# Convolutions moved behind the query/key pairs, temporaries in PSUM, rotations ahead of VectorE's low halves, h scaled pair by pair

## What is computed

```python
qk = jax.nn.silu(causal_conv(qk, c_conv_w[j], c_conv_b[j]))   # 2048 channels, 4 taps
lf = jax.nn.log_sigmoid(fg + c_b_f[j])
yc = mlstm(q, k, v, li, lf)
...
h = h + mix
pl = rmsnorm(p[i] @ ple_w[i], ple_norm[i])
h = h + jax.nn.sigmoid(h @ ple_gate_w[i]) * pl
...
return rmsnorm(h, final_norm)          # input of the second block, also its residual
# second block, both layers
q_b = apply_rope(qkv_b[:, :, 0], rot); k_b = apply_rope(qkv_b[:, :, 1], rot)
return x + (y @ w_out)
```

## Time and profile before

| | us |
|---|---|
| three timed runs | 2450.66, 2452.96, 2455.09 |
| their median | 2452.96 |
| the profiled execution | 2449.15 |
| its span, first to last instruction | 2447.4 |
| PE, POOL, DVE, ACT busy in it | 2223.3, 1801.4, 1354.6, 1230.6 |

### The profile page before, as it was taken

The page is one execution under the profiler, slowest core; times in us unless marked ns, Lnnn a source line. Parts: engine busy times, 40 slices in busy tenths (PEclk is TensorE's granted clock), DMA queues, the critical chain, the costliest instruction groups (busy, mean ns, idle before and its releaser), DMA issues.

```text
span 2447.4 us, 39060 instructions
## 1 busy us (share of the span) xinstructions
PE 2223.3 (91%) x12256; PEld 1899.9 (78%) x12256; DVE 1354.6 (55%) x1915; ACT 1230.6 (50%) x2192; POOL 1801.4 (74%) x1378
## 2 busy tenths in 40 slices
PE   6998885799997999879997889989999999998997
PEld 5887774688886788768886767778888888876886
DVE  6447687634538737774356765443742454258712
ACT  5454354456543455545564335334665544456654
POOL 6884466799877977669996955666679899854695
PEclk9999998899998999999998989999999999999998
DMA  7654332466654554435665433545456665643464
GB/s 241 191 169 121 91 104 68 147 189 190 182 178 140 173 176 134 125 121 168 188 197 153 148 100 114 156 150 160 142 172 188 181 193 172 190 123 109 138 174 135
DMA packets 211097, 378.92 MB, mean 155 GB/s; under 512 B 23440, under 2 KB 34320, under 8 KB 210832
## 3 DMA queue, kind: packets, MB, share of 16 engines
q1 hardware_dynamic: 205056, 363.95, 49.7%
q10 hardware_dynamic: 5904, 13.23, 1.5%
HBM read 374.99 MB, written 2.10 MB: 154 GB/s over the span
## 4 chain that ended last, share of the span: by engine, by line
PE 44%; POOL 20%; DVE 18%; issue 14%; ACT 3%; POOLq 0%; DVEq 0%; DMA 0%; ACTq 0%
PE ps L448 26%; POOL w_lo L401 20%; PE ps L449 13%; PE ps L530 1%; DVE ps L1361 1%; DVE tb L1360 1%; PE ps L698 1%; ACT w_hi L809 1%; DVE w L1366 1%; DVE ob L1602 1%; DVE w L1895 1%; DVE w L1533 1%; DVE w L1449 1%; PE ps L642 0%; DVE xa L1338 0%
## 5 line engine op out<-in xcount | busy, mean ns | idle before, releaser
L401 POOL TENSOR_TENSOR w_lo<-raw,w_hi 128x512 fp32r<-128x512 f32 (+1 forms) x1374 | 1801.2, 1332 | 624.8 <-ACT w_hi L809 586.9
L809 ACT ACTIVATE w_hi<-raw 128x512 fp32r<-128x512 f32 (+1 forms) x1420 | 854.2, 618 | 813.9 <-PE ps L449 761.8
L448 PE MATMUL ps<-xa,w_hi 128*128 128x512 f32 x2960 | 1077.9, 407 | 84.2 <-POOL w_lo L401 34.4
L449 PE MATMUL ps<-xa,w_lo 128*128 128x256 f32 x2960 | 838.2, 283 | 0.0
L448 PE MATMUL ps<-xb,w_hi 128*128 128x512 f32 x2160 | 768.4, 400 | 9.3 <-POOL w_lo L401 7.3
L448 PEld LDWEIGHTS ps<-xa,w_hi 128*128 128x128 f32 x2960 | 567.3, 192 | 232.4 <-POOL w_lo L401 31.9
L449 PE MATMUL ps<-xb,w_lo 128*128 128x256 f32 x2160 | 606.3, 281 | 0.0
L449 PEld LDWEIGHTS ps<-xa,w_lo 128*128 128x128 f32 x2960 | 570.5, 193 | 0.8
L448 PEld LDWEIGHTS ps<-xb,w_hi 128*128 128x128 f32 x2160 | 406.8, 188 | 110.5 <-POOL w_lo L401 8.2
L449 PEld LDWEIGHTS ps<-xb,w_lo 128*128 128x128 f32 x2160 | 409.5, 190 | 0.5
L1360 DVE TENSOR_SCALAR tb<-ps 128x512 f32<-128x512 f32 (+1 forms) x124 | 85.1, 686 | 389.1 <-PE ps L449 387.7
(11 more groups left out here) (307 smaller groups left out, 2086.5 us busy)
## 6 DMA issues: line engine op xcount, KB each, us to landing
raw<-w_gate_dram SPq DMA_DIRECT2D x128, 256.0 KB, 3.0
raw<-w_ogz_dram SPq DMA_DIRECT2D x128, 256.0 KB, 3.0
raw<-w_odin_dram SPq DMA_DIRECT2D x128, 256.0 KB, 3.0
raw<-w_evmoba_dram SPq DMA_DIRECT2D x112, 256.0 KB, 3.1
raw<-w_ein_dram SPq DMA_DIRECT2D x96, 256.0 KB, 3.1
raw<-w_evout_dram SPq DMA_DIRECT2D x80, 256.0 KB, 3.0
raw<-w_odgate_dram SPq DMA_DIRECT2D x72, 256.0 KB, 3.0
raw<-w_ein_zx_dram SPq DMA_DIRECT2D x64, 256.0 KB, 3.0
```

Of the source, the lines that this page charges most:

```text
L401: nc.gpsimd.tensor_tensor(w_lo[:, slot, 0:n], raw[:, at, 0:n], w_hi[:, slot, 0:n].bitcast(F32), SUB).then_inc(lo_pool, 1)
L448: mm(ps[:, bank + b, :], w_hi[:, slot, at], x[:, x0 + k, :], start=(k == 0), stop=False)
L449: ins = mm(ps[:, bank + b, 0:T], w_lo[:, slot, at], x[:, x0 + k, 0:T], start=False, stop=(k == st.blocks - 1))
L809: af(w_hi[:, slot, 0:n], raw[:, at, 0:n], ACT.Copy).then_inc(act_rounded, 1)
```

## The change

The squares of x are made two blocks at a time into PSUM banks 6 and 7, and added by DVE into `sq_sum`; ACT waits for these additions from the fourth on. ACT's eight DMA issues and the Exp for the parameters come later; the root of x comes before the parameter steps, and pair 3 of ein before the series. `root` keeps variance and temporary in PSUM bank 6, Newton has three operations in place of four, and `log1p` keeps two temporaries there, with one more copy. The convolution of a pair follows its take in oqk, with its accumulator in PSUM banks 4 and 5, its sigmoid behind unit 2 two pairs on, and its product behind the take of that pair; nothing of it is left in ov, where the Exp of the gates goes from unit 4 to unit 8. DVE makes no low half in oqk, one (unit 6) a pair in evmoba and odin from pair 2, and in both the rotation of pair p-2 comes first, then the low half, in odin the memory block, then the take. PE's wait for the variance before odin's second pair goes. The two multiplications of h go; in evout each pair of h is scaled by the kept root and `final_norm` in two operations ahead of its addition.

```diff
 LO_DVE = {
-    "oqk": (2, (3, 7)), "evmoba": (1, (3, 7)), "odmem": (0, (3, 7)),
+    "evmoba": (2, (6,)), "odin": (2, (6,)), "odmem": (0, (3, 7)),
 }
...
             def root(name, which):                                   # ACT
                 act.wait_ge(var_ready, ROOTS[name] + 1)
-                af(rs[:, which, :], tb[:, 0, :], ACT.Sqrt).then_inc(std_ready, 1)
+                af(rs[:, which, :], ps[:, 6, 0:T], ACT.Sqrt).then_inc(std_ready, 1)
...
-                if (p, q) in ((0, 5), (0, 7), (1, 0), (1, 1)):
-                    k = 4 * {5: 0, 7: 1, 0: 2, 1: 3}[q]
-                    af(w[:, k:k + 4, :], h[:, k:k + 4, :], ACT.Square).then_inc(sq_ready, 1)
-                if p == 1 and q == 2:
+                j = {(0, 5): 0, (0, 6): 1, (0, 7): 2, (1, 0): 3, (1, 1): 4, (1, 2): 5, (1, 3): 6, (1, 4): 7}.get((p, q))
+                if j is not None:
+                    if j > 2:
+                        act.wait_ge(sq_added, j - 2)
+                    af(spare(6 + j % 2) if j else sq_sum, h[:, 2 * j:2 * j + 2, :], ACT.Square).then_inc(sq_ready, 1)
+                if p == 1 and q == 4:
...
+                if q == 2 and not (isinstance(p, int) and p < 2):    # oqk, ACT
+                    conv_sigmoid(p - 2, par)
...
-            def conv_behind(p, par, q):
+            def mg_behind(p, par, q):                                # ov, ACT
                 if p == 0 and q == 4:
+                    conv_sigmoid(7, 1)
+                if p == 0 and q == 8:
                     act.wait_ge(mg_in, 1)
                     af(w[:, 36, :], w[:, 36, :], ACT.Exp, scale=-1.0).then_inc(mg_exp, 1)
-                if q in (7, 14):
-                    conv_sigmoid(2 * p + q // 14, q // 14)
...
             def newton(r, v, t, told=False):
-                step(tt(t, r, r, MUL))
-                step(tt(t, t, v, MUL))
-                step(ts(t, t, -0.5, 1.5, MUL, ADD))
+                step(tt(t, v, r, MUL))
+                step(stt(t, t, -0.5, r, MUL, MUL))
...
-                    step(tt(r, r, t, MUL))
+                    step(stt(r, t, 1.5, r, ADD, MUL))
...
-            def log1p(y, z, zz, p):
+            def log1p(y, zs, p):
+                n = y.shape[1]
+                z, zz = ps[:, 6, 0:n], ps[:, 6, T:T + n]
...
-                step(tt(zz, z, z, MUL))
+                step(ts(zs, z, 1.0, None, MUL))
+                step(tt(zz, z, zs, MUL))
...
-            for k in (4, 8, 12):
-                dve.wait_ge(sq_ready, k // 4 + 1)
-                step(tt(w[:, 0:4, :], w[:, 0:4, :], w[:, k:k + 4, :], ADD))
-            tt(w[:, 0:2, :], w[:, 0:2, :], w[:, 2:4, :], ADD).then_inc(sq_added, 1)
-            dve.wait_ge(sq_added, 1)
+            for j in range(1, 8):
+                dve.wait_ge(sq_ready, j + 1)
+                tt(sq_sum, sq_sum, spare(6 + j % 2), ADD).then_inc(sq_added, 1)
+                dve.wait_ge(sq_added, j)
+            root("x", RS_LAYER, D)
+            store("ein", w, 0, RS_LAYER, 0, 2)
...
-            root("x", RS_LAYER, D)
-            store("ein", w, 0, RS_LAYER, 0, 3)
+            store("ein", w, 0, RS_LAYER, 2, 3)
+            store("ein", w, 0, RS_LAYER, 3, 4, adding="mem", behind=2)
...
+            def oqk_pair(p, par):                                    # DVE
+                take(ST["oqk"], p, par, w[:, ds(p * 2, 2), :], RS_LAYER)
+                dve.wait_ge(pair_out, p + (STORED["oqk"] + 1))
+                if not (isinstance(p, int) and p < 2):
+                    silu(p - 2, par)
+                convolve(p, par)
+            for p in range(4):
+                oqk_pair(p, p % 2)
+            pairs_loop(dve, 8, oqk_pair, 4, steps=step, per=8)
+            store("ogate", w, 32, RS_LAYER)
+            silu(6, 0)
...
-                convolve(2 * p, 0)
-                if p:
-                    silu(2 * p - 1, 1)
-                convolve(2 * p + 1, 1)
-                silu(2 * p, 0)
...
-            root("first", RS_Q, D)
-            rf, rl, v = rs[:, RS_Q, :], rs[:, RS_LAYER, :], tb[:, 0, :]
-            step(tt(rl, rf, rf, MUL))
-            step(stt(v, ps[:, 7, T:2 * T], 1.0 / D, rl, MUL, MUL))
+            root("first", RS_FIRST, D)
+            rf, rl, v, t = rs[:, RS_FIRST, :], rs[:, RS_LAYER, :], ps[:, 6, 0:T], ps[:, 6, T:2 * T]
+            step(tt(v, ps[:, 7, T:2 * T], rf, MUL))
+            step(stt(v, v, 1.0 / D, rf, MUL, MUL))
...
-            step(tt(h[:, :, :], h[:, :, :], along(rf, 16), MUL))
-            step(tt(h[:, :, :], h[:, :, :], wide(col("final_norm"), 16), MUL))
...
                 def pair(p, par):                                    # results_pair
-                    dst = w[:, ds(p * 2, 2), :]
+                    if nb:
+                        rotate(p + (rope_at - 2), (rope_at + par) % 2, kind, p * 2 - 4, nb)
                     lower(st, p, par)
-                    take(st, p, par, dst, RS_LAYER)
                     if memory_behind:
                         split_gained("mem3", p, par, xb)
-                    if nb:
-                        dve.wait_ge(pair_out, p + STORED[name])
-                        rotate(p + (rope_at - 1), (rope_at + 1 + par) % 2, kind, p * 2 - 2, nb)
+                    take(st, p, par, w[:, ds(p * 2, 2), :], RS_LAYER)
+                    dve.wait_ge(pair_out, p + (STORED[name] + 1))
...
+                    if x_next:                                       # add_out
+                        for b in range(2):
+                            step.post(stt(hp[:, b:b + 1, :], hp[:, b:b + 1, :],
+                                          cols[:, ds(p * 2 + (COL_AT["final_norm"] + b), 1)],
+                                          rs[:, RS_FIRST:RS_FIRST + 1, :], MUL, MUL))
+                        step.wait()
                     a, b = halves_of(st, p, par)
```

More of the change, by code:

```diff
@@ L248, in build @@
         NORMS, n, m = {}, 0, 0
-        for name, squares, additions in (("x", 4, 1), ("mem", 8, 7), ("ple0", 2, 1), ("h1", 8, 7), ("ple1", 2, 1),
+        for name, squares, additions in (("x", 8, 7), ("mem", 8, 7), ("ple0", 2, 1), ("h1", 8, 7), ("ple1", 2, 1),
                                          ("first", 16, 14), ("cq", 2, 1), ("ckv", 1, 0), ("x3", 8, 7), ("last", 8, 7)):
@@ L1111, in conv_behind @@
                     af(small[:, 0:16], ps[:, 7, 0:16], ACT.Copy).then_inc(mg_gcols, 1)
-            stage("oqk", peel=2, behind=oqk_behind)
-            stage("ogate")
-            stage("ov", behind=conv_behind, peel=4)
+            stage("oqk", peel=4, behind=oqk_behind)
+            stage("ogate", behind=lambda p, par, q: conv_sigmoid(6, 0) if q == 2 else None)
+            stage("ov", behind=mg_behind, peel=4)
             stage("ogz", count=4, peel=4)
@@ L1180, in evc_behind @@
                 if (p, q) == (1, 3):
-                    root("first", RS_Q)
+                    root("first", RS_FIRST)
                 if (p, q) == (1, 6):
@@ L1775, in silu @@
                 dve.wait_ge(cv_sig, p + 1)
-                tt(w[:, ds(p * 2, 2), :], w[:, 38 + 2 * par:40 + 2 * par, :], sm[:, par, :, :], MUL).then_inc(cv_done, 1)
+                tt(w[:, ds(p * 2, 2), :], spare(4 + par), sm[:, par, :, :], MUL).then_inc(cv_done, 1)
                 dve.wait_ge(cv_done, p + 1)
+            def oqk_pair(p, par):
[9 more added lines that the diff above has]
+            silu(6, 0)
+            gx, gb, gm, t0, t1, t2 = (w[:, 32 + i, :] for i in range(6))
+            step(ts(gx, gx, col("c_gate_b"), None, ADD))
+            step(ts(t0, gx, 0.0, None, ALU.min))
+            stt(t1, gx, -1.0, gx, MUL, MAX).then_inc(mg_in, 1)
+            silu(7, 1)
+            dve.wait_ge(mg_exp, 1)
+            log1p(t1, t2, gm)
+            step(tt(t0, t0, gm, SUB))
+            step(ts(t2, t1, 0.0, 1.0, MUL, ADD))
+            nc.vector.tensor_tensor_scan(gb, t2, t0, 0.0, MUL, ADD).then_inc(mg_lf, 1)
+            dve.wait_ge(mg_lf, 1)
             sv = ST["ov"]
@@ L1805, in _ @@
             dve.wait_ge(mg_max, 1)
-            silu(7, 1)
             store("ogz", oa, 0, RS_LAYER, 0, 3)
@@ L2037, in add_out @@
                 pair(1, 1)
-                pairs_loop(dve, 8, pair, 2, steps=step, per=2 if x_next else 1, turn=st.turn)
+                pairs_loop(dve, 8, pair, 2, steps=step, per=4 if x_next else 1, turn=st.turn)
                 if not x_next:
@@ L2045, in _ @@
             dve.wait_ge(rope_loaded, 32 * 2)
-            results_pair("odin", 0, 0, 0, True)(0, 0)
-            pairs_loop(dve, 5, results_pair("odin", OD_ROT, 0, 2, True), 1, steps=step, per=5)
-            results_pair("odin", OD_ROT, 0, 1, True)(5, 1)
-            for p in (6, 7):
-                results_pair("odin", OD_ROT, 1, 2, True)(p, p % 2)
-            pairs_loop(dve, 12, results_pair("odin", OD_ROT, 1, 2), 8, steps=step, per=4)
-            store("odin", w, 0, RS_LAYER, 12)
+            for p in range(2):
+                results_pair("odin", memory_behind=True)(p, p)
+            pairs_loop(dve, 6, results_pair("odin", OD_ROT, 0, 2, True), 2, steps=step, per=5)
```

(4 more changed lines are left out.)

49 lines of the change are left out of this document (19 added, 30 removed).

## The result

The changed kernel took 2374.75 us as the median of four executions (2365.19 to 2376.40), the kernel before 2451.81 beside it. The ratio is 0.9678, its 95% interval 0.9648 to 0.9708. Run again later, five executions gave 2361.37 to 2374.10, median 2370.16, and a ratio of 0.9653 (0.9630 to 0.9676). The forecast was 2370.

What follows compares the result with a forecast made beforehand. TensorE was taken as the bound, busy 2223.3 of 2447.4 us, with VectorE behind its waits. Terms sum to 81.0, taking 2449.15 to 2368.2; the median was laid 1.8 above, at 2370, range 2358 to 2384.

Steps and rivals of the forecast that it cites:

- Start, 10.7: In ein: faster squares, root before parameter steps and pair 3 before the series shorten two PE waits and half clock; 10.7 us.
- Head norm, 2.2: One 128x2048 DVE step goes from the chain behind PE's wait of 11.39; 2.2 us.
- oqk, 3.0: Shorter h1 root, low halves to POOL, convolutions hidden on DVE, a new sigmoid stall near 0.6; 3.0 us gained.
- ov, 22.0: Convolutions leave ov, so it falls to 89.8; the late gate series costs nothing, or up to 5; 22.0 us gained.
- PE idle in front of the gate products: Sign of being wrong: PE waits after ov's first pair; that rival's late gates or sigmoids had chance 0.15.
- ogz, 2.5: Six PE waits ending a DVE chain with one Newton lose one step each; 2.5 us.
- evc, evmem and uq, 16.6: Shorter roots cut waits, the two whole multiplications of h go, and 2.9 of wait returns in evc; 16.6 us.
- the fourth rival: Scaling h pair by pair lands on the path in evout, costing 8 x 2.8 at most: 2392 us; chance 0.04.
- evmoba, 22.1: DVE owes only unit 6, so PE's wait before unit 3 goes and eight pairs take 96.6; 22.1 us.
- slower rival: Rotation ahead of DVE's low half makes unit 6 late in evmoba and odin; at 3.5 late, 2460 us; chance 0.02.
- odin and end, 1.9: Shorter root in odin gives 1.6 and the last root 0.3; 1.9 us.
- The PSUM rival: PSUM temporaries don't help, so an oqk pair costs DVE 14.1 against 11.1; 2406 us; chance 0.04.

Runs made afterwards that it cites:

- the first trace: Changed kernel, nothing altered: the profiled execution of its first four, 2365.19 us, the fastest of them.
- the second trace: Changed kernel, nothing altered, traced once more: 2374.10 us.
- the single line in the kernel before: Kernel before the change with DVE's low halves in oqk and evmoba cut, POOL making all: 2429.38 us, ratio 0.9907.
- the first two experiments: Changed kernel with convolution accumulator in SBUF: 2388.79 us; with root temporaries in SBUF: 2383.65 with three Newton operations, 2400.26 with four.

## Why the prediction was right, step by step

**Start, 10.7.** The stage gained 10.9, but by other steps than I gave. The order was said to bring 1.2 at the root and, with PSUM, the 4.1 of the second wait; undone, it costs neither. The first wait came out as forecast, 2.25 for 2.2. ACT's moved DMA issues cost a wait of 1.18 in the second pair; the unit with it took 3.60 us for 1.39, so 2.2 in all, more than the 1.5 allowed.

**Head norm, 2.2.** Ein_zb gained 2.2, the sum of two things: PE's wait fell by 4.3 (11.39 to 7.13), more than the one 128x2048 step, and PE's busy time in the stage rose by 1.8, at a clock of 0.86 for 0.89. That the two leave just the 2.2 is luck.

**oqk, 3.0.** It gained 1.4 in the first trace, 2.6 in the second. The stall at the first sigmoid was 0.7 to 0.9 (the two units there against their usual length) for the 0.6 forecast, and moving the sigmoids two units on removes it. The price of a switch on the Trainium skill's page ScalarE: Activation LUTs (What ACT_TABLE_LOAD costs) had made it 2.0; the trace doesn't agree. The rest is pace: seven of the eight pairs of the first trace ran at 1.413 a unit.

**ov, 22.0.** This is the step that failed in size: 17.2 and 20.4 in the two traces. The convolutions went as counted. The step that failed is "27 us after oqk, when PE has finished ov's first pair at 27.9. It costs nothing": the series ended at 742.2, 29.6 us after oqk, and PE, through at 740.4, waited 1.82. DVE's timeline at the end of the series:

```profile
734.71 1.79 DVE L1482 SCALAR_TENSOR_TENSOR w<-w,ps 128x256 f32<-128x256 f32 x4
736.53 0.42 DVE L1483 SCALAR_TENSOR_TENSOR w<-w,ps 128x256 f32<-128x256 f32 x1
736.99 0.79 DVE L1484 TENSOR_SCALAR w<-w 128x256 f32<-128x256 f32 x1
737.81 1.40 DVE L1789 TENSOR_TENSOR w<-w 128x256 f32<-128x256 f32 x1
739.25 1.27 DVE L1790 TENSOR_SCALAR w<-w 128x256 f32<-128x256 f32 x1
740.55 1.64 DVE L1791 TENSOR_TENSOR_SCAN w<-w 128x256 f32<-128x256 f32 x1
```

The polynomial, with its factor in PSUM, takes 0.45 a step; the last four operations, left in SBUF, take 5.1 while POOL works. The first three of them are 3.46 where the likes of them in the earlier trace rows take 0.29, 0.42 and 0.29 at best: 2.5 lost, more than the wait. By the rule of the Trainium skill (VectorE: DVE Perf Modes, Why PSUM operands drop a tier) the prediction put the danger in the PSUM operands; the measured loss lies in the operations that stayed in SBUF. Another cause stands earlier in the same series, and no run separates the two: DVE sat idle for ACT's Exp, which now stands behind unit 8 and has a table load of 1.28 in front.

```profile
728.32 0.43 DVE L1475 TENSOR_SCALAR ps<-w 128x256 f32<-128x256 f32 x1 [1.57 <-ACT w L1111]
```

That the late series is what ov lacks is shown: with the gate products behind four more units the stage is 89.3 for the 89.8 forecast. Behind the wait of 1.82 the first trace has 6.8 us at half clock, the second none: 3.3 of difference that I hadn't in the sum. The 5 that I allowed "if it is late" covers both. "PE idle in front of the gate products" was among the signs of being wrong, and it came.

**ogz, 2.5.** 1.9 in the first trace, where the six waits fell by 2.3; in the second, with its two stretches at half clock, the stage is 1.3 longer than before the change. Ov and ogz together gained 18.9 in both traces, for 24.5 forecast, and 24.3 with the gate products later. The sign "Newton steps at 0.42 to 0.48 everywhere" doesn't hold here: those of ogz stayed in SBUF and take up to 1.40.

**evc, evmem and uq, 16.6.** Measured 6.1, 9.7 and 2.4, or 18.2 (evc 4.2 in the second trace, with half clock behind the wait). The wait that comes back in evc's third pair is 2.53 for 2.9. Undoing the scaling alone returns evmem's 9.3 and shows that evout hides its substitute: the fourth rival is refuted.

**evmoba, 22.1.** 22.5; eight pairs 96.5 for 96.6. The reason given, one low half for two, is all of it, as the run in the old order and the single line in the kernel before show. The rotation's new place gains nothing there, and would cost 14.5 if the two low halves stayed. My slower rival had that mechanism right; what it needs is a low half that is wanted before rotation and take are through, and unit 6 isn't one.

**odin and end, 1.9.** Odin 2.6. Further stages gained without being forecast (evout 2.1, ukv 2.7, evgate_a 1.0). Evout's is pace alone, and the second trace has neither it nor more than 0.4 of ukv's: these gains are the execution's more than the change's.

The PSUM rival fell with the first two experiments; it would have been 2406. Undone together, place and fourth operation are worth some 27 us, and the convolution's place some 16, by one execution each.

The sum was 81.0, the two spans differ by 84.4; against the later medians, 2453.53 and 2370.16, the change gives 83.4, against the first ones 77.1. That the misses in ov and oqk and the unforecast gains cancel is luck of some 5 us.

## What to carry to other kernels

Count an engine's spare time per unit before giving it a share of another's work: POOL had room for all of it, and one line of the table of low halves was over a quarter of the whole gain (24.4 of 83.4). Put one operand of each small dependent VectorE operation in PSUM where GpSimd works in SBUF all the time, and look for the ones left over: here they stand at the end of the chain, right in front of the wait that is left. Before reordering for a short series, see whether the engine waits at that place anyway.

## What was not expected of the hardware

PE has two paces at full granted clock for the same 3072 columns a unit, 1.387 and 1.413 us, and often keeps one for a whole stage; it may change where small products or a wait come between. Gate0, with identical instructions, in the run with two low halves:

```profile
533.20:623.60 90.40, 90.40 (x513) 78.46 (x512) 43.58 (x73) 53.91 (x94) 81.35 (x65) 1.00 0.60 185
```

90.4 against 88.7 above, no idle time and clock 1.00 in both. Evout is 114.7 or 116.9 in the same way. Of some 1015 units that show one pace or the other from start to start, 472 were slow in the first trace of the changed kernel and 723 in the run without low halves: 251 x 0.026 = 6.5 of the 13.4 us between these two executions. In the second trace, 9 us longer than the first, 479 were slow: the pace isn't all that differs. What picks it wasn't tried.

And the same wait of 1.82 us was followed by 6.8 us at half clock once and by none another time; that trace had its half clock in ogz instead, some 165 us later. The wait of 2.53 in evc left that stage at 38.8 in the first trace and at 40.7, with a mean clock of 0.96, in the second. From these two waits I put the price behind a short wait between nothing and 3 us, as an estimate; only the wait itself can be forecast.
